# Slot tables by indirect DMA in a two-layer hybrid trunk with a mixture of experts

## The reference, cut to what matters

```
def grouped_moe(h, router_w, router_b, w_g, w_u, w_d):
    s = sigmoid(h @ router_w);  sb = (s + router_b) in 4 groups of 4
    grp  = argmax over groups of the sum of the best two sb
    eidx = the two best experts inside grp
    w    = s[eidx] / sum(s[eidx]);  gates = w at eidx, 0 elsewhere
    for e in range(16):
        a = silu(h @ w_g[e]) * (h @ w_u[e])        # 1024 -> 512
        y = y + gates[:, e:e+1] * (a @ w_d[e])     # 512 -> 1024
    return y

x  = x + gate1 * (merged @ w_out)
h2 = rms_norm(x) * (1 + scale2) + shift2
x  = x + gate2 * grouped_moe(h2)
```

## Time and profile before

| what | us |
|---|---|
| median of 3 runs (lowest, highest) | 1665.41 (1663.58, 1669.59) |
| the profiled execution | 1667.87 |
| its span in the profile | 1666.1 |
| PE busy (of the span) | 1579.4 (95%) |
| DVE busy | 1072.4 (64%) |
| ACT busy | 925.8 (56%) |
| POOL busy | 513.1 (31%) |

### The profile page before, as it was taken

How to read it: one execution, slowest core, us unless ns; L and a number is a source line. 1 busy time by engine, 2 the same in 40 slices (tenths; PEclk the granted TensorE clock), 3 DMA queues, 4 the chain that set the end, 5 groups by cost and what they waited for, 6 DMA issues and landing times.

```text
span 1666.1 us, 21627 instructions
## 1 busy us (share of the span) xinstructions
PE 1579.4 (95%) x7771; PEld 1244.3 (75%) x7771; DVE 1072.4 (64%) x1519; ACT 925.8 (56%) x1284; POOL 513.1 (31%) x253
## 2 busy tenths in 40 slices
PE   7999999999998999999889999999999999999996
PEld 4677778777775788888766777777777677888884
DVE  2235636753345999999862355476533589999997
ACT  3434444445344788888644343444353568888882
POOL 2344554344520011111234444444344111111112
PEclk9999999999998999999989999999999999999998
DMA  9855343344358999999946543433443479999994
GB/s 363 288 190 164 101 130 99 89 139 143 114 191 318 344 360 369 360 364 359 374 158 214 171 154 110 130 89 89 140 141 114 172 267 374 365 365 367 362 359 161
DMA packets 153311, 381.70 MB, mean 229 GB/s; under 512 B 20612, under 2 KB 26374, under 8 KB 153212
## 3 DMA queue, kind: packets, MB, share of 16 engines
q1 hardware_dynamic: 122704, 325.32, 56.3%
q10 hardware_dynamic: 20140, 36.56, 6.2%
q0 software_dynamic: 10368, 18.51, 3.0%
HBM read 378.52 MB, written 27.89 MB: 244 GB/s over the span
## 4 chain that ended last, share of the span: by engine, by line
PE 77%; DVE 10%; DMA 7%; ACT 4%; issue 2%; POOL 0%; SPq 0%; ACTq 0%; DVEq 0%; POOLq 0%
PE ps L598 62%; PE ps L607 5%; PE ps L631 2%; DVE wxl L2438 2%; PE ps L944 2%; DMA raw<-w_e_down 1%; DMA raw<-w_e_up 1%; DMA own<-w_mod 1%; PE ps L972 1%; PE ps L878 1%; ACT wxh L1822 1%; DVE uv L2213 1%; ACT wh L1327 1%; PE ps L642 1%; PE ps L650 1%
## 5 line engine op out<-in xcount | busy, mean ns | idle before, releaser
L1945 POOL TENSOR_TENSOR wl<-raw,wh 128x1024 fp32r<-128x1024 f32 x168 | 408.4, 2435 | 535.9 <-ACT wh L1327 535.7
L2438 DVE TENSOR_TENSOR wxl<-raw,wxh 128x1024 fp32r<-128x1024 f32 x384 | 462.1, 1221 | 43.2 <-ACT wxh L1822 31.8
L1822 ACT ACTIVATE wxh<-raw 128x1024 fp32r<-128x1024 f32 x384 | 405.3, 1059 | 101.8 <-PE ps L598 66.1
L598 PE MATMUL ps<-wxh,xeT 128*128 128x512 f32 x1024 | 349.3, 403 | 3.8 <-issue 2.6
L1327 ACT ACTIVATE wh<-raw 128x1024 fp32r<-128x1024 f32 x168 | 176.6, 1055 | 229.2 <-PE ps L598 223.5
L598 PE MATMUL ps<-wh,hTh 128*128 128x512 f32 x720 | 294.5, 409 | 7.1 <-DVE hTl L2060 4.5
L598 PE MATMUL ps<-wh,hTl 128*128 128x512 f32 x720 | 282.9, 393 | 0.0
L598 PE MATMUL ps<-wl,hTh 128*128 128x512 f32 x720 | 282.5, 392 | 0.0
L598 PEld LDWEIGHTS ps<-wxh,xeT 128*128 128x128 f32 x1024 | 194.5, 190 | 45.1 <-issue 4.0
L598 PE MATMUL ps<-wxl,xeT 128*128 128x512 f32 x512 | 201.0, 393 | 0.0
L598 PEld LDWEIGHTS ps<-wh,hTh 128*128 128x128 f32 x720 | 136.4, 189 | 42.0 <-issue 7.1
(11 more groups left out here) (264 smaller groups left out, 2209.4 us busy)
## 6 DMA issues: line engine op xcount, KB each, us to landing
raw<-w_e_gate SPq DMA_DIRECT2D x128, 512.0 KB, 6.0
raw<-w_e_up SPq DMA_DIRECT2D x128, 512.0 KB, 5.5
raw<-w_e_down SPq DMA_DIRECT2D x128, 512.0 KB, 5.4
raw<-w_in SPq DMA_DIRECT2D x120, 512.0 KB, 3.8
own<-w_mod ACTq DMA_DIRECT2D x27, 1024.0 KB, 7.9
raw<-w_mod SPq DMA_DIRECT2D x36, 512.0 KB, 5.0
raw<-w_br_b SPq DMA_DIRECT2D x16, 512.0 KB, 3.8
raw<-w_out SPq DMA_DIRECT2D x16, 512.0 KB, 3.7
```

What stands on the lines that cost most here:

```text
L598: ins = pe.matmul(out, act_hl[i], w_hl[j], start=start and n == 0, stop=stop and n == 2)
L1822: act.activation(wxh[:, q % RING_MOE, :, :], raw[:, place, :, :], ACT.Copy).then_inc(sem("hi_done"), 1)
L1945: pool.tensor_tensor(wl[:, p % RING, :, :], raw[:, PAIR_CHUNK[p] % RAW, :, :], wh[:, p % RING, :, :].bitcast(F32), ALU.subtract).then_inc( ...
L2438: dve.tensor_tensor(wxl[:, q % RING_MOE, :, :], raw[:, expert_chunk(l, 0, q)[0], :, :], wxh[:, q % RING_MOE, :, :].bitcast(F32), ALU.subtr ...
```

## The change: what it does

- A table in device memory, `table_rows`, has for each slot of each expert the token's row and the row of its output. POOL fills it with "no token" early in each layer. DVE computes for each token the places of its two experts in that table (`table_row`), in seven small instructions behind the router's third pick (and in the first layer four more that write the constant `table_data`). POOL writes the 384 tokens' two entries by six indirect DMAs of 128 rows of 8 bytes, and reads the table back into `slot_table` by one DMA.
- Experts 0 to 2 keep picks and token sums. For experts 3 to 15 both are gone from PE and DVE; the gather and the scatter read their rows from `slot_table`. The gather of expert e waits for `xe_ready` in place of `idx_ready`. `own_gate` no longer computes `slot_dest` for them.
- Expert 15's down product goes to banks 6 and 7 in place of 4 and 5, and no longer waits until DVE has read expert 14's. The combined units use other banks (bank 0 twice).
- DVE's three adds of the read-back parts are spread: tile 0 before the flag, tile 1 between the halves of expert 15's output, tile 2 after two combined units.
- Names of semaphores, the body behind the flag, and two more instructions at POOL's start follow from this.

```diff
+PICKED = 3
-LAST_BANKS = (6, 7, 0, 1, 2, 3)
+LAST_BANKS = (0, 1, 2, 3, 5, 0)
...
+    table_rows = nc.dram_tensor("table_rows", (P * NE, 2), I32).ap()
+    table_slots = table_rows.rearrange("(p e) c -> p (e c)", e=NE)
...
-                    j, bank = (2 * (i % 2) + n, 4 + i // 2) if halves else (i, 4 + n)
+                    j, bank = (2 * (i % 2) + n, 6 + i // 2) if halves else (i, 4 + n)
...
-                        if i == 1 and not (late and e + 3 >= NE):
-                            token_sums(e + 3, k + 3, ps[:, 1, 0:2])
...
-                            if not (late and e + 3 >= NE):
-                                pe.wait_ge(sem("idx_ready"), at("idx_ready", l, 4) + e)
...
-                if last:
-                    pe.wait_ge(sem("out_ready"), at("out_ready", l, 1))
-                elif not is_expert(e, 0):
+                if not last and not is_expert(e, 0):
...
+                if LAST_BANKS[u] in LAST_BANKS[:u]:
+                    pe.wait_ge(sem("comb_done"), at("comb_done", l, LAST_BANKS.index(LAST_BANKS[u]) + 1))
...
+            pool.dma_start(table_slots, no_token[:, :]).then_inc(sem("table"), 16)
...
-                pool.wait_ge(sem("idx_ready"), at("idx_ready", l, 1) + e)
+                if e < PICKED:
+                    pool.wait_ge(sem("idx_ready"), at("idx_ready", l, 1) + e)
+                    index = slot_index[:, e:e + 1]
+                else:
+                    pool.wait_ge(sem("xe_ready"), at("xe_ready", l, e))
+                    index = slot_table[:, e, 0:1]
...
-            for e in range(3):
+            for e in range(2):
                 fetch_rows(e, e)
+            pool.wait_ge(sem("table"), at("table", l, 16))
+            pool.wait_ge(sem("slot_done"), at("slot_done", l, 2))
+            for t in range(NT):
+                for s in range(2):
+                    pool.indirect_dma_start(table_rows[:, :],
+                                            bass.IndirectOffsetOnAxis(ap=table_row[:, t, s:s + 1], axis=0),
+                                            table_data[:, t, s, :], None,
+                                            bounds_check=last_slot, oob_is_err=False).then_inc(sem("table"), 16)
+            fetch_rows(2, 2)
+            pool.wait_ge(sem("table"), at("table", l, 16 * (2 * NT + 1)))
+            pool.dma_start(slot_table[:, :, :].rearrange("p e c -> p (e c)"), table_slots).then_inc(sem("table"), 16)
+            pool.wait_ge(sem("table"), at("table", l, 16 * (2 * NT + 2)))
...
             def turned_pick(e, k):
 
+                dve.wait_ge(sem("table"), at("table", l, 16 * (2 * NT + 2)))
+                link(dve.tensor_copy(slot_token[:, k, 0:1], slot_table[:, e, 0:1]))
...
-                if more_picks and not is_expert(e, 0):
-                    make_pick(e + 3, k + 3)
                 expert_lo(e, 14)
                 act_lo(e)
                 expert_lo(e, 15)
-                if more_picks:
-                    slot_rows(e + 3, k + 3, ps[:, 1, 0:2])
...
+            link(dve.scalar_tensor_tensor(place3, slot[:, :, :], float(NE), iota[:, 0:NE].unsqueeze(1).to_broadcast([P, NT, NE]),
+                                          ALU.mult, ALU.add))
+            link(dve.tensor_tensor(first3, place3, mask[:, 0:NT, :], ALU.mult))
+            link(dve.tensor_tensor(second3, first3, gate[:, :, NE:2 * NE], ALU.mult))
+            link(dve.tensor_reduce(rt[:, 3, 0:3], first3, AX.X, ALU.add))
+            link(dve.tensor_reduce(rt[:, 3, 3:6], second3, AX.X, ALU.add))
+            dve.tensor_tensor(table_row[:, :, 0], rt[:, 3, 0:3], rt[:, 3, 3:6], ALU.subtract)
+            link(dve.tensor_copy(table_row[:, :, 1], rt[:, 3, 3:6]))
+            dve.sem_inc(sem("slot_done"), 1)
...
-            for t in range(NT):
+            def add_parts(t):
+
                 dve.wait_ge(sem("parts_added"), at("parts_added", l, t + 1))
                 link(dve.tensor_tensor(y[:, t, :], y[:, t, :], gbc[:, 1, min(t, 1), :], ALU.mult))
                 link(dve.tensor_tensor(x[:, t, :], x[:, t, :], y[:, t, :], ALU.add))
+
+            add_parts(0)
...
+            last_lo(0)
+            add_parts(1)
+            last_lo(1)
             for u, (t, half) in enumerate(LAST_UNITS):
                 cols = slice(half * W, (half + 1) * W)
+                if u == 2:
+                    add_parts(2)
```

More of the change, by code:

```diff
@@ L329, in build @@
     slot_dest = place("slot_dest", [P, 4], I32)
+    slot_table = place("slot_table", [P, NE, 2], I32)
+    no_token = place("no_token", [P, NE * 2], I32)
+    table_row = place("table_row", [P, NT, 2], I32)
+    table_data = place("table_data", [P, NT, 2, 2], I32)
     slot_index = place("slot_index", [P, 4], I32)
@@ L1287, in turn @@
                 for t in range(NT):
-                    last = transpose(ps[:, 6, t * P:(t + 1) * P], pick1[:, t, :])
+                    last = transpose(ps[:, 4, t * P:(t + 1) * P], pick1[:, t, :])
                 last.then_inc(over_pe, 1)
@@ L1293, in turn @@
                 for k in range(4):
-                    last = transpose(ps[:, 7, k * P:(k + 1) * P], ae[:, k * P:(k + 1) * P])
+                    last = transpose(ps[:, 5, k * P:(k + 1) * P], ae[:, k * P:(k + 1) * P])
                 last.then_inc(over_pe, 1)
@@ L1904, in scalar_program @@
                 act.wait_ge(sem("pair_used"), used_at(l, NE - 1, HEAD + 1 + 2 * half))
-                act.activation(oes[1][:, 0, half * W:(half + 1) * W], ps[:, 4 + half, :], ACT.Identity,
+                act.activation(oes[1][:, 0, half * W:(half + 1) * W], ps[:, 6 + half, :], ACT.Identity,
                                scale=slot_gate[:, k:k + 1]).then_inc(sem("out_hi"), 1)
@@ L1966, in scatter_rows @@
                 name = f"scattered{k % 2}"
+                index = slot_dest[:, e:e + 1] if e < PICKED else slot_table[:, e, 1:2]
                 pool.wait_ge(sem("out_hi"), at("out_hi", l, 1) + e)
                 pool.indirect_dma_start(part_rows[:, :],
-                                        bass.IndirectOffsetOnAxis(ap=slot_dest[:, k % 4:k % 4 + 1], axis=0),
+                                        bass.IndirectOffsetOnAxis(ap=index, axis=0),
                                         oe_rows[k % 2][:, :], None,
@@ L2460, in own_gate @@
                 dve.tensor_copy(slot_gate[:, k % 4:k % 4 + 1], xg[:, k % 2, bass.ds(e + D, 1)])
-                if not (isinstance(e, int) and e < 4):
-                    name = f"scattered{k % 2}"
-                    dve.wait_ge(sem(name), (e - k % 2) * 8 + at(name, l, -16))
+                if not (isinstance(e, int) and e < PICKED):
+                    return
                 dve.tensor_scalar(slot_dest[:, k % 4:k % 4 + 1], xg[:, k % 2, bass.ds(e + (D + NE), 1)], 0.5,
@@ L2532, in vector_program @@
             make_pick(2, 2)
+            if l == 0:
+                for s in range(2):
+                    dve.tensor_scalar(table_data[:, :, s, 0], tokens_r[:, :, 0].bitcast(F32), float(NO_TOKEN), None, ALU.add)
+                    dve.tensor_scalar(table_data[:, :, s, 1], tokens_r[:, :, 1].bitcast(F32), float(NO_TOKEN + s), None, ALU.add)
+            place3, first3, second3 = [rt[:, i, 0:48].rearrange("p (t e) -> p t e", t=NT) for i in range(3)]
+            link(dve.scalar_tensor_tensor(place3, slot[:, :, :], float(NE), iota[:, 0:NE].unsqueeze(1).to_broadcast([P, NT, NE]),
[7 more added lines that the diff above has]
+            dve.sem_inc(sem("slot_done"), 1)
             if l + 1 < DEPTH:
@@ L2615, in vector_program, with last_lo @@
             k = (NE - 1) % 4
-            for half in range(2):
+            def last_lo(half):
                 dve.wait_ge(sem("out_hi"), at("out_hi", l, NE + half))
                 cols = slice(half * W, (half + 1) * W)
-                dve.scalar_tensor_tensor(oes[1][:, 1, cols], ps[:, 4 + half, :], slot_gate[:, k:k + 1],
+                dve.scalar_tensor_tensor(oes[1][:, 1, cols], ps[:, 6 + half, :], slot_gate[:, k:k + 1],
                                          oes[1][:, 0, cols].bitcast(F32), ALU.mult, ALU.subtract).then_inc(sem("out_ready"), 1)
+            last_lo(0)
+            add_parts(1)
+            last_lo(1)
             for u, (t, half) in enumerate(LAST_UNITS):
                 cols = slice(half * W, (half + 1) * W)
+                if u == 2:
+                    add_parts(2)
                 dve.wait_ge(sem("comb_acc"), at("comb_acc", l, COMBINED - 5 + u))
```

33 lines of the change are left out of this document (19 added, 14 removed).

## The result

The changed kernel took 1646.11 us (median of 4 runs, 1640.41 to 1647.76), the kernel before beside it 1664.49 us (4 runs, 1660.76 to 1669.59): ratio 0.987, 95% interval 0.9842 to 0.9898 (the two medians alone give 0.989). Faster, as forecast, but by 18.4 us in the medians where 13.7 was worked out; the profiled executions differ by 1667.87 - 1647.76 = 20.1 us.

A forecast was written before the change was run, and what follows sets the result against it. PE was taken to set the loop's pace, with the DMA engines some 2% behind. 6.5 + 1.9 + 0.6 + 5.7 - 1.0 = 13.7 us off 1665.4 gave 1651.7, said as 1652; range 1643 to 1663.

The forecast's parts named there:

- Token sums leave PE: Expert loop, experts 3 to 15: 26 groups of 0.31 us leave PE's list; 6.5 us saved, bounds 0 and 8.1.
- The weights' floor: Expert loop: weight loads, at a ceiling of 372 GB/s, allow no round under 17.95 us.
- Picks leave DVE: Expert loop: PE's 5.6 us of waits for picks go, a third kept as gain; 1.9 us, bounds 0 and 5.6.
- The clock behind a stop: Expert loop: the round after a 1.88 us stop ran at clock 0.91, costing 1.7 us; a third, 0.6 us, saved.
- The table's making: DVE's small instructions behind the third pick, covered while the first gather lands; cost 0, at most 4 us uncovered.
- writing: POOL's six indirect writes of the table beside weight prefetch; cost 0.5 us a layer, 1.0 in all.
- The third rival: Table writes on POOL's queue hold up the third gather beyond 20.0 us for all six; slower, to 1702.9 us; chance 10%.
- The layer's end: After the expert loop: waits filled or gone, 4.1 us in layer 0 and 1.6 in layer 1; 5.7 us, bounds 3 and 7.
- The first rival: Expert loop: DMA engines already set the pace, rounds stay at 18.2 us; 1660.7 us; chance 20%.
- The second rival: DMA engines have room, so sums, picks, clock and ends come whole, 21.1 us; 1644.3 us; chance 15%.

The follow-up runs named there:

- e1: Changed kernel with PE's token-sum matmuls for experts 3 to 15 put back, waiting for nothing and read by nobody; ratio 0.989 to the kernel before.
- e11: Changed kernel with PE's token sums and DVE's picks and copies put back, neither engine waiting for the other; ratio 0.9883 to the kernel before.
- e14: Changed kernel with sums and picks put back, DVE waiting for sums and PE for DVE's copies, but PE not for picks; ratio 0.9877 to the kernel before.
- e9: Changed kernel with four matmuls of each round left out for experts 1 to 15, same loads, casts and waits; ratio 0.9859 to the kernel before.
- e13: Changed kernel with sums and picks put back and, of the waits between PE and DVE, only PE's for the pick; ratio 0.9941 to the kernel before.
- e4: Changed kernel with the six table writes done twice, the second time into a table nobody reads; 1650.64 us against 1649.82 for the changed kernel.
- e10: Kernel before with the tables made, written and used, but old picks, token sums, waits and layer's end kept; ratio 0.9994 to the kernel before.
- e2: Changed kernel with the layer's end of the kernel before put back (banks 4 and 5, adds in one row); ratio 0.9918 to the kernel before.
- e15: The changed kernel again, unchanged, for reference; ratio 0.9867 to the kernel before.

## Why the prediction was right in direction and short in size

- *Token sums leave PE*, 6.5 us within 0 to 8.1: mis-sized, and for the wrong reason. The step of 0.31 us was too small (a round lost 0.43: 0.35 for the group with the matmuls that it splits, 0.08 for the wait for the pick). But the sums alone, put back without waits, cost at most 4 us, and in the traces show in layer 1 only (e1, e11, e14).
- *The weights' floor* of 17.95 us a round, from 365 / 0.98: wrong. 371 to 380 GB/s were moved at shares of 0.98 to 1.01. The Trainium skill's rate of 425 GB/s ("DMA: Bandwidth & Descriptors", "Measured (HBM→SBUF, 128 partitions, SWDGE, issued from GpSimd)"), by which 15.7 us would do, an estimate, isn't reached either: with a shorter list (e9) the loops stayed as long, at 362 and 374 GB/s.
- *Picks leave DVE*, 1.9 + 0.6 us, a third of what the rows had: this is the step that failed. I argued that PE, without its wait, would meet DVE's late `wxl` a little later. It doesn't. Without the wait PE stands nowhere for it (0.2 us for a `wxl` in layer 0's loop of the kernel after, none in e11's), and the stops go whole: 5.6 us of PE's waits for picks in the earlier trace rows, 6.2 in e13, plus 26 x 0.08 = 2.1 us for rounds of 18.23 in place of 18.15, make 7.7 to 8.3 us; e13 against e14 and e11 measured 9.7 to 10.7. My argument reads a wait as something that only moves. Here the pick stood behind the sixth `wxl`, and the stop that it caused early in the loop came on top of a list in which PE has no other gap to make it up (the rounds of e11 and e13). That the stop lets the weights run ahead until ACT's buffers are full (92 waits for PE) is argued from the waits, not shown apart.
- *The clock behind a stop*, 0.6 of 1.7 us: the price fits the one stop that it was read from. Its window of 18.34 us is no full round; from sums to sums that round lasts 587.44 - 567.56 = 19.88 us, 1.65 over 18.23, and the granted clock was 0.57 from 567.60 to 571.60. But not every stop brings it: behind e13's stop of 2.21 us it was 1.00 (562.60 to 566.60).
- The errors of the sums' term (6.5 us for at most 4) and of the picks' (2.5 for some 10) partly cancel, so it is in part luck that the total came as near as it did.
- *The table's making*, 0, and *writing*, 1.0 us: right, even double (e4, e10). The third rival, POOL's queue, was off: 12.9 us for six writes, under its point of 20.0, and even 22.5 us for twelve did no harm, since that gather has more room than I gave it.
- *The layer's end*, 5.7 us (3 to 7): right in sum. The traces give 4.7 in the first pair and, in the mean of three old and eleven changed ends, 54.0 - 48.1 = 5.9; e2 5 to 8.5. Inside, layer 0 gave 2.7 for 4.1 because PE's first unit was late by its jump, which I hadn't priced for PE, and layer 1 gave 2.0 for 1.6.
- *The first rival* (weights set the pace, so nothing of the loop comes) had a bound right and its consequence wrong: the loads do bound the loop now, beside PE's list, but near 17.8 us a round and not at 18.2. *The second rival* (all of it comes, 1644.3) came nearest in time, 1.8 us off.

## What to carry to other kernels

A wait that stands in the pacing engine's list costs more than its share of the busy time: price it by putting the work back without the wait and the wait without the rest, as e11 and e13 do. Before halving a stop because "it only moves", ask whether the engine has any slack behind it in which to make it up. And take no transfer ceiling from a busy share, and no bound from the count of waits alone: it tells which side is ahead. Shortening one engine's list (e9) and lengthening it (e11) told the bounds of this loop.

## What the runs showed of the hardware

- Three matmuls of 2 columns between matmuls of 512 cost PE 0.35 us a group (rounds of 18.15 in e11 and 17.8 in e15), though their step in the chain is 0.23 in e1: the neighbours take 0.11 us more.
- An indirect write of 128 rows of 8 bytes cost POOL 1.3 us of issue where it was quick (1.0 busy and 0.30 between) and up to 2.3, and twelve in a row landed 22.5 us after the first began.
- PE's first matmul behind a jump came up to 5.9 us late where loads of 512 KB had just been issued, 0.25 to 0.42 where they were held, and at most 0.15 us late in layer 1; in the late cases it began 1.2 to 1.7 us behind a 16 KB packet of an instruction queue.
